# Joining a residual update and the next norm over 512 tokens in a two-block transformer kernel

## The reference, cut to what matters

```
y = mixer(...)                       # or conv_ffn(...), linear output, 1024 wide
x = x + g1 * rmsnorm(y, norm_g[i, 1])
h = modulate(rmsnorm(x, norm_g[i, 2]), sh2, sc2)   # rmsnorm * (1 + sc2) + sh2
... = h @ w_in
```

## Time and profile before

| what | value |
|---|---|
| median of 3 runs | 1987.7 us (1986.43 to 1993.09) |
| the profiled run's own time | 1983.22 us |
| its span | 1981.5 us |
| TensorE busy (matmul) | 1891.4 us, 95% |
| VectorE busy | 1239.0 us, 63% |
| ScalarE busy | 913.7 us, 46% |
| GpSimd busy | 228.8 us, 12% |
| mean granted TensorE clock | 0.989 |

### The profile page before, as it was taken

One profiled execution on the slowest core, in us unless ns is written; L12 is line 12 of the kernel. 1 busy time (PEld: TensorE's weight loads), 2 busy tenths in 40 slices (PEclk: granted clock), 3 DMA queues, 4 the chain that ended last, 5 costly groups with the idle time before them and its releaser, 6 DMA issues.

```text
span 1981.5 us, 33458 instructions
## 1 busy us (share of the span) xinstructions
PE 1891.4 (95%) x13373; PEld 1681.3 (85%) x13373; DVE 1239.0 (63%) x1865; ACT 913.7 (46%) x1429; POOL 228.8 (12%) x179
## 2 busy tenths in 40 slices
PE   5999989999999899999989998999999999989998
PEld 3776657778888589999979997998999999879997
DVE  6355465543654646667587767656975667787564
ACT  5344353322332422168465654347654445665453
POOL 2100104430542000022000000000000010000001
PEclk9999999999999999999999999999999999999999
DMA  9611465433222533232435553532455554224553
GB/s 384 248 64 64 168 236 191 163 116 114 89 89 89 191 119 116 86 107 86 170 141 180 207 178 136 172 130 89 142 173 188 172 178 142 96 96 171 192 192 128
DMA packets 43951, 296.79 MB, mean 150 GB/s; under 512 B 4976, under 2 KB 6128, under 8 KB 11696
## 3 DMA queue, kind: packets, MB, share of 16 engines
q1 hardware_dynamic: 36576, 247.48, 36.1%
q10 hardware_dynamic: 6048, 42.50, 5.9%
q0 software_dynamic: 1200, 5.02, 0.7%
HBM read 293.94 MB, written 1.05 MB: 149 GB/s over the span
## 4 chain that ended last, share of the span: by engine, by line
PE 82%; DVE 10%; ACT 4%; issue 2%; DMA 1%; POOL 1%; DVEq 0%; ACTq 0%; POOLq 0%
PE acc L466 23%; PE acc L467 22%; PE acc L468 22%; DVE w_lo L401 2%; PE acc L461 2%; PE acc L463 2%; PE acc L462 2%; PE wk L559 2%; PE wk L1768 1%; ACT w_hi L391 1%; PE acc L1757 1%; PE wk L1497 1%; DVE X L1108 1%; DVE nt L1114 1%; PE acc L1518 1%
## 5 line engine op out<-in xcount | busy, mean ns | idle before, releaser
L401 DVE TENSOR_TENSOR w_lo<-w_raw,w_hi 128x1024 fp32r<-128x1024 f32 (+2 forms) x472 | 574.1, 1255 | 182.1 <-ACT w_hi L391 180.7
L391 ACT ACTIVATE w_hi<-w_raw 128x1024 fp32r<-128x1024 f32 (+2 forms) x472 | 452.5, 1005 | 415.8 <-PE acc L468 320.4
L466 PE MATMUL acc<-Hhi,w_hi 128*128 128x272 f32 (+2 forms) x1936 | 616.9, 319 | 14.4 <-DVE Hlo L891 6.8
L467 PE MATMUL acc<-Hlo,w_hi 128*128 128x272 f32 (+2 forms) x1936 | 600.0, 310 | 0.0
L468 PE MATMUL acc<-Hhi,w_lo 128*128 128x272 f32 (+2 forms) x1936 | 599.8, 310 | 0.0
L466 PEld LDWEIGHTS acc<-Hhi,w_hi 128*128 128x128 f32 x1936 | 365.5, 189 | 59.1 <-issue 31.7
L468 PEld LDWEIGHTS acc<-Hhi,w_lo 128*128 128x128 f32 x1936 | 365.7, 189 | 19.3
L467 PEld LDWEIGHTS acc<-Hlo,w_hi 128*128 128x128 f32 x1936 | 365.9, 189 | 17.8
L466 PE MATMUL acc<-Fhi,w_hi 128*128 128x256 f32 (+2 forms) x864 | 262.1, 303 | 3.3 <-POOL Flo L1187 1.6
L467 PE MATMUL acc<-Flo,w_hi 128*128 128x256 f32 (+2 forms) x864 | 261.3, 302 | 0.0
L468 PE MATMUL acc<-Fhi,w_lo 128*128 128x256 f32 (+2 forms) x864 | 261.2, 302 | 0.0
(11 more groups left out here) (432 smaller groups left out, 2820.9 us busy)
## 6 DMA issues: line engine op xcount, KB each, us to landing
w_raw<-in_w_ffn_in SPq DMA_DIRECT2D x44, 1024.0 KB, 4.8
ada_ring<-in_w_ada ACTq DMA_DIRECT2D x40, 1024.0 KB, 5.4
w_raw<-in_w_mlp_in SPq DMA_DIRECT2D x32, 1024.0 KB, 4.8
w_raw<-in_w_mlp_out SPq DMA_DIRECT2D x32, 1024.0 KB, 4.8
w_raw<-in_w_ffn_out SPq DMA_DIRECT2D x32, 704.0 KB, 4.0
ada_first<-in_w_ada SPq DMA_DIRECT2D x8, 1024.0 KB, 20.1
w_raw<-in_w_ret_v SPq DMA_DIRECT2D x8, 1024.0 KB, 4.8
w_raw<-in_w_ret_g SPq DMA_DIRECT2D x8, 1024.0 KB, 4.7
```

Source lines behind the costliest of these rows:

```text
L391: act.activation(w_hi[:, r, a:b], w_raw[:, r, a:b], ACT.Copy).then_inc(hi_done, 1)
L401: dve.tensor_tensor(w_lo[:, r, a:b], w_raw[:, r, a:b], w_hi[:, r, a:b].bitcast(F32), ALU.subtract).then_inc(lo_done, 1)
L466: pe.matmul(o, w_hi[:, r, w], x_hi(k), start=k == 0, stop=False)
L467: pe.matmul(o, w_hi[:, r, w], x_lo(k), start=False, stop=False)
```

## The change

1. **Residual and norm are joined over 512 tokens.** With r the reciprocal root of y's mean square and G the gate, the new sum of squares is that of x + r*G*y, which is sum(x*x) + 2 r sum(G*x*y) + r*r sum(G*G*y*y). While the output matmuls run, ScalarE also scales `Y` by the gate in place and squares it again (`act_y_gated`), and VectorE multiplies it with X and adds both products up over the chunks (`dve_y_products`). The three sums are packed in one PSUM bank. `dve_residual_norm` forms the new sum in four small operations on 128x128 tiles, so the second root comes from `x_sum` and not from the new X. Then one loop does, for each chunk, X's update two chunks ahead, the norm's product, and `H_lo`. All chunks are now scaled by ScalarE.
2. **The ada groups move.** Groups 3 to 8 of the nine go from the stretch between the norms into the next projection's first slot, one ahead of each k from 1 to 6; after `ffn0` the closing matmuls move from k = 4 to k = 7. ScalarE's ring loads 6 and on are issued in the norm's loop.
3. **First weights ahead.** The splits of the next projection's slot 1 are done inside the norm (`following`), also in part at the norm before `ffn1_in0`.
4. **Second feed-forward.** `act_ffn_in_alone` and `dve_ffn_in_alone` finish the gate chunk before they touch the up chunk, and split the output projection's slot 1 ahead of the last hidden chunk (`ahead=True` in the output projection skips it).
5. **The opening** sums the squares of the input once more in packed form and keeps them as `x_sum`.
6. **The end.** VectorE scales all eight chunks, SP stores the even and ScalarE the odd ones.

```diff
+        def dve_residual_norm(dve, r, following):
+            j, (layer, g) = r + 1, RES[r][3]
+            dve.wait_ge(yroot_ready, r + 1)
+            dve.reciprocal(fold[:, 1, :], fold[:, 0, :]).then_inc(yrstd_ready, 1)
...
+            dve.tensor_tensor(fold[:, 2, :], wk[:, 1, P:2 * P], fold[:, 1, :], ALU.mult).then_inc(y_steps, 1)
+            dve.scalar_tensor_tensor(fold[:, 2, :], wk[:, 1, 0:P], 2.0, fold[:, 2, :], ALU.mult, ALU.add).then_inc(y_steps, 1)
+            dve.tensor_tensor(fold[:, 2, :], fold[:, 2, :], fold[:, 1, :], ALU.mult).then_inc(y_steps, 1)
+            dve.tensor_tensor(x_sum[:, :], x_sum[:, :], fold[:, 2, :], ALU.add).then_inc(nsq_used, DC)
...
+            dve.wait_ge(spread, 2 * r + 1)
+            scaled(0)
+            dve.wait_ge(root_ready, j + 1)
+            dve.reciprocal(rstd[:, 0:P], root_of(j)).then_inc(rstd_ready, 1)
+            update(0)
+            scaled(1)
+            update(1)
+            dve.wait_ge(spread, 2 * j)
+            for c in range(DC):
+                dve.tensor_tensor(nt[:, c % 2, :], X[:, c, :], wk[:, 1, :], ALU.mult).then_inc(nt_ready, 1)
+                if c + 2 < DC:
+                    scaled(c + 2)
+                if c >= 1:
+                    dve_norm_low(dve, j, c - 1)
+                if c + 2 < DC:
+                    update(c + 2)
+                if c == DC - 2:
+                    split_lo(dve, Step(proj[following], None, 0), (0,))
+            dve_norm_low(dve, j, DC - 1)
+            split_lo(dve, Step(proj[following], None, 0), (1,))
...
+            dve.tensor_tensor(nt[:, 0, :] if m else xy_acc[:, :], X[:, m, :], Y[:, m, :], ALU.mult).then_inc(y_steps, 1)
...
+            dve.tensor_tensor(gy_acc[:, :], gy_acc[:, :], n32[:, m % 2, :], ALU.add).then_inc(y_steps, 1)
+            dve.tensor_tensor(xy_acc[:, :], xy_acc[:, :], nt[:, 0, :], ALU.add).then_inc(y_steps, 1)
...
+        def act_y_scale(act, r, m):
+            for g, a, b in y_gate(r, m):
+                ins = act.activation(Y[:, m, a:b], Y[:, m, a:b], ACT.Identity, scale=g)
...
+            out0 = Step(p.next, None, 0)
+            split_hi(act, out0, (0,))
             high(p.n - 1)
+            split_hi(act, out0, (1,))
...
-            pe_norm(pe, 1, between=lambda c: pe_ada(pe, ADA_OUT + 4 + c // 2) if c in (1, 3, 5) else None)
+            def first_need(k):
+                if 1 <= k <= 6:
+                    pe_ada(pe, ADA_OUT + 2 + k)
+                h_need(pe, j)(k)
...
+        def store_out(eng, odd):
+            for c in range(odd, DC, 2):
```

More of the change, by code:

```diff
@@ L649, in act_out_scaled, with act_plain @@
             rest(p.n)
-        def act_plain(act, name, meanwhile={}, after=None):
+        def act_plain(act, name, meanwhile={}, after=None, ahead=False):
             def slot(st):
-                split_hi(act, st)
+                if not (ahead and st.i is None and st.s == 0):
+                    split_hi(act, st)
                 if meanwhile:
                     meanwhile[st.s]()
-            each_slot(act, proj[name], slot, after=after)
+            each_slot(act, proj[name], slot, peel=ahead, after=after)
         def dve_plain(dve, name, after=None):
@@ L827, in act_norm, with dve_norm_low @@
                 act.activation(hi[:, c, 0:n], n32[:, c % 2, 0:n], ACT.Copy).then_inc(hhi_ready, 1)
[L829 removed]
+                if c >= 2:
+                    act_ada(act, ada + 1 + c, ada + 2 + c)
+        def dve_norm_low(dve, j, c):
             n, x0, groups, gain, shift = NORMS[j]
[L831 to L869 removed]
@@ new lines, in stack_kernel @@
+        Y_SQUARE, Y_USED, Y_STEP = (0, 3 * DC, 6 * DC, 7 * DC), (0, DC + 2, 2 * DC + 4, 3 * DC + 4), {}
+        y_count = 0
+        for r in (0, 1):
+            for m in range(DC):
+                for step in ("out", "product", "gated", "added"):
+                    if (step != "out" or (r == 0 and m % 2 == 0)) and (step in ("out", "product") or m < DC - 1) \
+                            and (step != "added" or m >= 1):
+                        y_count += 1
+                        Y_STEP[r, step, m] = y_count
+            for step, count in (("sum", 3), ("scaled", DC)):
+                for i in range(count):
+                    y_count += 1
+                    Y_STEP[r, step, i] = y_count
@@ L1032, in dve_y @@
+        def dve_y(dve, name, add=None, tail=None, ahead=False):
             p = proj[name]
@@ L1035, in slot @@
             def slot(st):
-                split_lo(dve, st)
+                if not (ahead and st.i is None and st.s == 0):
+                    split_lo(dve, st)
                 if tail and st.s == 0:
@@ L1056, in act_y_squares @@
                 st = Step(p, None, s)
-                split_hi(act, st)
+                if s > 0 or not ahead:
+                    split_hi(act, st)
                 if during:
@@ L1135, in slot @@
             def slot(st):
-                split_hi(act, st)
+                if layer or half or st.i is not None or st.s:
+                    split_hi(act, st)
                 f, r = st.s + f0, st.parity()
@@ L1246, in dve_ffn_in_alone @@
[L1246 to L1251 removed]
+                left(st, 0)
+                right(st, 0)
                 if s >= 1:
```

395 lines of the change are left out of this document (255 added, 140 removed).

## The result

| kernel | median of its runs | beside the kernel before, same chip | ratio, 95% interval |
|---|---|---|---|
| changed | 1978.58 us (10 runs, 1970.04 to 1984.76) | 1989.32 us (10 runs) | 0.9935 (0.9917 to 0.9954) |

The change made the kernel faster, by 0.0065 x 1989 = 12.9 us, between 9.1 and 16.5 (the two medians differ by 10.7). The forecast was 15.8 of gain and 1971.9 us; the time is inside the range and 6.7 above the forecast. The profiled execution of the changed kernel is the slowest of its ten: its own time is 1984.76 us against 1983.22 before, although the seams in it are shorter. So the two traces are compared stage by stage and not by their spans.

The account below looks back on a forecast made before the run. TensorE bounds the kernel (82% of the chain), so only its waits can pay. Gains 7.4 + 5.5 + 1.0 + 1.9 = 15.8 from the median 1987.7 give 1971.9 us, range 1968.5 to 1981.

Parts of the forecast that it names:

- the first rival: First slots after both norms: TensorE is the bound, through half clock or late ring loads; gain 8 to 13, chance 0.20.
- First seam: From `hyb_out`'s last chunk to `ffn0_in0`: last `Hlo` complete at 287.6 against 294.99, 7.4 us gained.
- Fold operations: Four new VectorE operations on 128x128 tiles in the joined norm: about 0.3 us each, 1.2 in all, showing as 0.1.
- Loop and tail: VectorE's norm loop over chunks 0 to 6, 16.2 us, then chunk 7 to the last `Hlo`, 3.24 us.
- six ada groups now stand in the first slot: First slot after the norm: groups and matmuls take TensorE 11.9 of 16 us, so 4 are spare.
- Second seam: After `ffn0_out1`, the same norm work: ends at 690.1 against 695.61, 5.5 us gained.
- VectorE's slower list: Rival in the norm loops: dependent operations cost 0.9 in place of 0.60 us; gain 0 to 8, chance 0.10.
- The second root: Rival in the norm: the second root still waits for something late, such as ScalarE, costing 1 to 3 us a seam.
- The output slots of `ffn0_out1`: VectorE and ScalarE's loop takes 7.3 of a 7.48 us slot; rival that it bounds the slots and slows the kernel, 0.03.
- Second feed-forward: Output projections' second slots: `w_lo` comes earlier, the last hidden low half 0.5 later; 0.5 us each, 1.0 gained.
- The end: Final scaling by VectorE alone and stores from two queues: last store out at 1977.5 against 1979.41, 1.9 us gained.
- Opening: Kernel start: four more small matmuls, about 0.4 us, hidden before a load wait of 1.1; net 0.

Follow-up runs that it names:

- the two repeats: The changed kernel run again unaltered, twice: medians 1979.06 and 1979.96 us, each 0.9946 of the kernel before.
- runs 4: The changed kernel with 7 further unused matmuls behind each norm's spread, run twice: 0.9923 and 0.9932 of the kernel before, medians 1969.43 and 1976.12 us.
- 1: The changed kernel with three of each first slot's six ada groups moved ahead of k = 0: 0.9923 of the kernel before, median 1974.05 us.
- 8: Changed kernel unaltered twice (0.9946 each), three ada groups ahead of k = 0 again (0.9924), and that with 3 matmuls ahead of each spread (0.9918).
- run 5: The changed kernel with three groups ahead of k = 0 and VectorE's chunk 6 operations behind the last copy: 0.993 of the kernel before, 1970.54 us.
- run 6: The changed kernel with first slots of `ffn0_in0` and `ret_k` done chunk after chunk: 0.9974 of the kernel before, median 1978.94 us.
- second run of 4: Repeat of the changed kernel with 7 further unused matmuls behind each norm's spread: 0.9932 of the kernel before, median 1976.12 us.

## Why the prediction was right, and where it was off

The direction, the range and most steps held. The size of the seams did not, and with 12.9 the gain lies just under the 13 to 18 that the forecast was given, among the 8 to 13 of the first rival. That it came so near is partly luck: the two repeats give 10.8 each, and the terms as the traces show them add up to 8.8 of the 15.8.

*First seam, 7.4 forecast, 4.2 measured.* By its own steps, from a copy on time (260.96) to the end of the last `Hlo` (291.63) it is 30.7 in place of 28.3. "The last chunk leaves on time": no, 0.9 late, behind the products for chunk 6. First product 5.5 after the copy: 4.7, so 0.8 back. Fold operations 0.3 each: 0.29. Start of the loop 3.4: 3.5. Loop and tail 19.4: 21.6, so 2.2 lost. Together 2.4 lost and 5.0 kept. Then TensorE begins k = 7 about 1.0 after the last `Hlo`, where before it began it at once, which leaves 4.0; the stage shows 4.2.

The step that failed is "six ada groups now stand in the first slot: 6 x 1.07 = 6.4 of TensorE beside 8 x 0.68 of matmuls, 11.9 in the 16 us". The matmuls beside the loop are 48 and not 24: 8 x 1.4 = 11.1, and with the groups 17.5 and their starts 18, more than the loop's 16.2 and the 16.95 that it took. So there was nothing to spare in the first slot, where the prediction had 4 us, and TensorE was its bound: everything that it lost showed, the half clock first of all. By the seams of runs 4, 1 and 8 the half clock cost 1.9 us and the groups' own time about 0.5. With three groups less in that stretch the predicted 19.4 came out to 0.1, and the seam gained 6.3 to 6.5. What is missing to 7.4 even then is k = 7, which TensorE still begins 1.0 after the last `Hlo`. The copy's 0.9 and the 0.8 given back cancel, and moving VectorE's work out of the copy's way (run 5) gained nothing.

*Second seam, 5.5 forecast, 2.3, 3.6 and 2.3 measured.* The same with a longer half clock: loop and tail 22.2, and the closing matmuls at 690.88, 1.5 us behind the end of the last `Rlo`, forecast 0.3. The copy is 0.9 late, forecast 0.8. Without the half stretch it gained 5.0, with the groups ahead 5.2 to 5.7, the forecast.

*The rivals.* "TensorE is the bound in the first slots" is what happened, given 0.20, with the forecast of gains of 8 to 13. It named the half clock and late loads as the causes. Late loads held nothing up in the changed kernel. The half clock is there and is the larger part of what was lost: 1.6 and 2.6 us of the first slots. It shows only because TensorE's plain work fills the loop, which I had excluded by a miscount; with the count that I had (run 6, second seam) the loop was as short as forecast in spite of it. The Trainium skill (TensorE: Matmul & The Clock Gate, Part 1) has the clock fall when TensorE idles and come back under sustained activity, and the runs agree as far as they go: a granted clock of 0.50 around the 4.5 us of standing, in both seams of all six profiles that have this wait, 1.00 all along in the second run of 4, which stands 1.8 and 1.6 us. But where it falls differs between executions of the same code. VectorE's slower list fell: 0.60 an operation held throughout. The second root was in time: its reciprocal follows the first product without a wait. The output slots of `ffn0_out1` stayed at 7.48, as forecast.

*Second feed-forward, 1.0 forecast, 0.6 to 0.7 measured:* `w_lo` no longer holds TensorE up, but in either half the last `Flo` can, by more than the 0.5 that the prediction allowed in two of the first halves and two of the second. *The end, 1.9 forecast, 1.4 measured:* the issue saved 2.0, landing took 0.6 of it, which the prediction had as equal. *Opening, 0:* 0.3 lost where the half stretch stands at 28 us as before, 1.7 where it stands at 38; the four small matmuls aren't the 1.7.

The terms as measured in the traces, with the means over the three profiles of the changed kernel, are 4.0 + 2.7 + 0.7 + 1.4 = 8.8. The timed runs give 12.9, 10.8 and 10.8, each uncertain by 3 to 4. They don't contradict, but 2 to 4 us of the timed gain have no place in a trace that I could find; that stays open.

## What to carry to other kernels

When work is moved under the shadow of another engine's loop, add up that engine's whole list per step, and read the number of instructions per step off the timeline (here six matmuls for each k, visible in the trace of before) and not off a description of the loops. When two engines hand buffers back and forth inside a loop, the wait that the profile shows on one of them may be only the echo of the other being full: shift the wait, and see if the end moves. Put work with early inputs into an engine's idle stretch before the loop, so that a half stretch falls on work that nothing waits for. When a forecast counts on slack to hide a cost, check the slack first: in run 6 the half clock didn't lengthen the second seam's loop, and in the changed kernel it was the larger part of the loss.

## What the runs showed of the hardware

*Two paces of the same matmuls.* In stages with 256 columns TensorE starts a matmul every 0.113 or every 0.118 us, for whole projections, at a granted clock of 1.00 and with no wait, in the same code. One window of 36 us in `mlp1_out0`, in the changed kernel and in its repeat (lines view: count, busy us, mean ns, idle us; the granted clock is 1.00 in both):

```profile
L471 PE MATMUL acc<-Flo,w_hi 128*128 128x256 f32 x103 | 29.0, 281 | 0.0
```

```profile
L471 PE MATMUL acc<-Flo,w_hi 128*128 128x256 f32 x107 | 29.5, 276 | 0.0
```

A projection of 384 matmuls takes 45.23 or 43.52 us, `ffn1_in1` 62.19 or 59.84. Of 14 profiles 6 had the slow pace in `mlp1_in0` and 6 in `ffn1_in1`, the unaltered changed kernel in one or the other of the two in each of its three profiles; the kernel before, profiled once, had it in neither, and the changed kernel's first profile in `ffn1_in0` and `mlp1`. It mostly changes where TensorE has waited, and in some profiles inside `ffn1_in0` without a wait. Three projections of the last feed-forward make 5.0 us of difference, a third of what lies between the fastest and the slowest of the ten runs. Its cause is open, and since it comes and goes in the same code, two single traces can't be compared by their spans to better than that.

*The half clock* doesn't fall at the same places in each execution of the same code. In the second seam it lasted from 667 to 677 us in two profiles of the changed kernel and from 667 to 673 in the third, which alone moved the seam's gain from 2.3 to 3.6. In the opening, which is the same in all 13 profiles other than before's, it stood at 28 us or was absent in eight, with 57.5 to 58.2 us to `hyb_qk0`, and at 38 to 44 us in five, with 59.3 to 61.8. Before has it at 28, and 57.8.
